# The first third of a modulation matrix walked by column halves, with a query projection cut in two around it

## The reference, cut to what matters

```
mod = silu(cond) @ w_ada + b_ada              # cond: 2 rows (prompt, sample); w_ada: 2048 x 12288
sh1, sc1, gt1, sh2, sc2, gt2 = split(mod, 6)  # 2048 columns each
h = rmsnorm(x, g_pre_mix) * (1.0 + sc1) + sh1
proj = h @ w_in                               # q, k, v, g, decay ranks, hyena inputs
q = proj[:, 0:512]
```

## Time and profile before

| | us |
|---|---|
| three runs | 1532.54, 1532.09, 1527.59 |
| median | 1532.09 |
| profiled execution, its own time | 1530.56 |
| its span | 1528.7 |
| PE busy in the span | 1379.7 (90%) |
| DVE busy | 748.8 (49%) |
| ACT busy | 241.7 (16%) |
| DMA moved | 422.19 MB |
| mean granted TensorE clock | 0.965 of full speed |

### The profile page before, as it was taken

How to read it: one execution, slowest core, us unless ns; L and a number is a source line. 1 busy time by engine, 2 the same in 40 slices (tenths; PEclk the granted TensorE clock), 3 DMA queues, 4 the chain that set the end, 5 groups by cost and what they waited for, 6 DMA issues and landing times.

```text
span 1528.7 us, 14045 instructions
## 1 busy us (share of the span) xinstructions
PE 1379.7 (90%) x5198; PEld 630.9 (41%) x5198; DVE 748.8 (49%) x1269; ACT 241.7 (16%) x401; POOL 75.1 (5%) x126
## 2 busy tenths in 40 slices
PE   2679999999999989999999999889989888798977
PEld 0135544444555545555544444543333333333322
DVE  0139889998677687978693752530000000000006
ACT  2110320100011111211121101521111101111104
POOL 3010000000001000000000001000000000000001
PEclk9689999999999999999999999989999999999999
DMA  9998458777549643322215844589999999999996
GB/s 345 424 359 254 170 173 276 249 259 254 165 144 339 222 146 109 117 69 90 83 55 213 289 157 170 235 351 427 427 426 394 430 427 428 426 386 427 427 424 279
DMA packets 134032, 422.19 MB, mean 276 GB/s; under 512 B 10253, under 2 KB 76024, under 8 KB 116852
## 3 DMA queue, kind: packets, MB, share of 16 engines
q1 hardware_dynamic: 120292, 375.79, 64.3%
q0 software_dynamic: 7584, 33.38, 6.0%
q10 hardware_dynamic: 6096, 12.20, 2.2%
HBM read 407.96 MB, written 22.58 MB: 282 GB/s over the span
## 4 chain that ended last, share of the span: by engine, by line
PE 74%; DMA 11%; DVE 8%; issue 3%; ACT 2%; ACTq 0%; POOL 0%; DVEq 0%; SPq 0%; POOLq 0%
PE ps L503 19%; PE ps L506 19%; PE ps L892 13%; PE ps L912 7%; DMA s_mem<-in_w_exp_gate 4%; PE ps L777 3%; DMA s_mem<-in_w_ada 3%; DMA s_mem<-in_w_exp_down 2%; DVE s_mem L1766 2%; PE ps L450 2%; PE ps L674 1%; DMA s_mem<-in_hy_freq 1%; PE ps L625 1%; PE ps L432 1%; DVE s_mem L1738 1%
## 5 line engine op out<-in xcount | busy, mean ns | idle before, releaser
L1592 DVE SCALAR_TENSOR_TENSOR s_mem<-s_mem,s_sT 128x512 f32<-128x512 f32 x480 | 339.4, 748 | 32.6 <-DMA s_mem<-in_w_ada 16.2
L503 PE MATMUL ps<-s_mem 128*128 128x384 f32 x1024 | 342.5, 492 | 1.1 <-DVE s_mem L1623 1.1
L506 PE MATMUL ps<-s_mem 128*128 128x512 f32 x672 | 292.8, 594 | 0.7 <-ACT s_mem L1366 0.7
L892 PE MATMUL ps<-s_mem 128*64 128x512 f32 x1152 | 256.4, 602 | 19.9 <-DMA s_mem<-in_w_exp_gate 18.7
L503 PEld LDWEIGHTS ps<-s_mem 128*128 128x128 f32 x1024 | 193.3, 191 | 142.5 <-issue 18.0
L506 PEld LDWEIGHTS ps<-s_mem 128*128 128x128 f32 x672 | 126.3, 190 | 158.5 <-issue 157.6
L892 PEld LDWEIGHTS ps<-s_mem 128*64 128x64 f32 x1152 | 87.4, 139 | 185.9 <-issue 185.9
L2059 DVE TENSOR_TENSOR s_mem<-s_mem,ps 64x512 f32<-64x512 f32 x18 | 12.2, 679 | 296.3 <-ACT s_mem L1461 296.3
L912 PE MATMUL ps<-s_mem 128*64 128x512 f32 x576 | 144.2, 659 | 9.3 <-DVE s_mem L2061 9.3
L1262 ACT ACTIVATE s_mem<-ps 128x512 f32<-128x512 f32 (+1 forms) x61 | 34.4, 581 | 316.3 <-PE ps L506 154.0
L912 PEld LDWEIGHTS ps<-s_mem 128*64 128x64 f32 x576 | 43.7, 150 | 96.4 <-issue 84.6
(11 more groups left out here) (287 smaller groups left out, 1025.0 us busy)
## 6 DMA issues: line engine op xcount, KB each, us to landing
s_mem<-in_w_ada SPq DMA_DIRECT2D x256, 256.0 KB, 3.2
s_mem<-in_w_exp_gate SPq DMA_DIRECT2D x32, 2048.0 KB, 21.1
s_mem<-in_w_exp_up SPq DMA_DIRECT2D x32, 2048.0 KB, 25.4
s_mem<-in_w_exp_down SPq DMA_DIRECT2D x32, 2048.0 KB, 24.4
s_mem<-in_w_in SPq DMA_DIRECT2D x24, 2048.0 KB, 8.8
s_mem<-in_w_ada SPq DMA_DIRECT2D x16, 2048.0 KB, 12.5
s_mem<-in_w_out SPq DMA_DIRECT2D x8, 2048.0 KB, 8.2
y_slots<-s_mem ACTq DMA_DIRECT2D x34, 256.0 KB, 11.1
```

Source lines behind the costliest of these rows:

```text
L503: m = mm(ps[:, banks[m_], 0:TOK], v[:, k, m_ * P:(m_ + 1) * P], hT[:, kk, :], start=(kk == 0), stop=(kk == KT - 1))
L506: m = mm(ps[:, banks[m_], :], hT[:, kk, m_ * P:(m_ + 1) * P], v[:, k, :], start=(kk == 0), stop=(kk == KT - 1))
L892: m = mm(ps[half, 0, :], hgT[:, kh * 8 + k, :], weights(e, 2 * kh + which)[:, k, :], start=(kh + k == 0), stop=(kh * 8 + k == KT - 1), ski ...
L1592: v.op(ve.scalar_tensor_tensor(out=o, in0=w, scalar=scale, in1=o, op0=ALU.mult, op1=ALU.add), S("piece_used") if last else None)
```

## The change

The first third of `w_ada` is loaded as 16 blocks of 512 rows by 1024 columns, so 4 KB in a piece per row instead of 16. The first eight (`ada_step(0, i)`) hold columns 0 to 1023 of scale and of shift, alternating, and complete the modulation of channel tiles 0 to 7; the second eight (`ada_step(1, i)`) do tiles 8 to 15. A step still has 8 matmuls of 32 columns.

The row work on DVE is replaced: ACT copies the sums out of PSUM (`ada_copy`), PE brings them into columns with 16 matmuls of 128x32 against a constant (`ada_columns`), and DVE adds bias and gain there in three small instructions and modulates 8 tiles (`modulate`).

The first half of the query projection (8 of 16 channel tiles, 32 matmuls) is spread among the second eight steps, from buffers of its own (`wq`); the second half (32 matmuls) follows `ada_columns(1)`. SP issues the two query blocks after ring loads 7 and 12. Eight pieces of the later thirds are issued after ring loads 9 to 15, and 12 steps of `ada_steps` run before `modulate(1)`. Before the decay ranks there are now 12 + 4 + 2 steps on DVE instead of 26; six of the steps taken away return inside GLA heads 0, 1 and 3 (two each) and two before the heads. ACT's queue now issues the condition rows and x first and the filter MLP's small inputs after them.

The core of the diff:

```diff
-            slot = i % RING if i < KT else (i - KT + 1) % 2
+            slot = i % RING if i < 8 else i % 2
...
+        Q_LOAD_AFTER = {7: 0, 12: 1}
...
+            def ada_step(g, i):
+                r, q = i // 2, (SCALE, SHIFT)[i % 2]
+                cols = q * D + g * 2 * NCOL
+                w = next_slot(pe, w_ada[4 * r * P:4 * (r + 1) * P, cols:cols + 2 * NCOL].rearrange("(k p) n -> p k n", p=P))
...
+            for i in range(4, 8):
+                for kt in range(4 * (i - 4), 4 * (i - 3)):
+                    x_turn(kt)
+                ada_step(0, i)
...
+            ada_columns(0)
+            pe.wait_ge(S("in_q0"), 16)
+            for m_ in range(4):
+                take(pe, m_, f"q_{m_}", ("act",))
+                if m_ < 3:
+                    q_products(m_, range(8))
+                    ada_step(1, 2 * m_)
+                    ada_step(1, 2 * m_ + 1)
+            q_products(3, range(2))
+            ada_step(1, 6)
+            q_products(3, range(2, 4))
+            ada_step(1, 7)
+            q_products(3, range(4, 6))
+            ada_columns(1)
+            q_products(3, range(6, 8))
+            pe.wait_ge(S("in_q1"), 16)
+            for m_ in range(4):
+                q_products(m_, range(8, KT)).then_inc(filled(f"q_{m_}"), 1)
...
-            run(26)
...
+            modulate(0)
+            sine_argument("hid2", 1, P)
+            run(12)
+            modulate(1)
+            run(4)
+            run(2)
...
-            run(4)
+            run(6)
...
-                    run((2, 1, 2, 1, 1, 1, 2, 2)[event])
+                    run((2, 2, 2, 2, 1, 1, 2, 2)[event])
```

More of the change, by code:

```diff
@@ L77, in shape_constants @@
     lower = (np.arange(P) >= BLK)[:, None]
-    base = np.concatenate([ident, tri, sel.reshape(P, 2 * P), total, np.tile(rows, (P, 1)), tokens, lower], 1).astype(np.float32)
+    conds = np.zeros((P, 2, 32), np.float32)
+    for j in range(4):
+        for c in range(2):
+            conds[32 * j + c, j // 2, c] = 1
+    base = np.concatenate([ident, tri, sel.reshape(P, 2 * P), total, np.tile(rows, (P, 1)), tokens, lower, conds.reshape(P, 64)], 1).astype(np.float32)
     masks = np.zeros((P, 2, P), np.int32)
@@ L435, in ada_sum, with ada_columns @@
                 mi.then_inc(filled(key), 1)
[L437 to L454, removed]
+            def ada_step(g, i):
+                r, q = i // 2, (SCALE, SHIFT)[i % 2]
+                cols = q * D + g * 2 * NCOL
+                w = next_slot(pe, w_ada[4 * r * P:4 * (r + 1) * P, cols:cols + 2 * NCOL].rearrange("(k p) n -> p k n", p=P))
+                bank, key = (6 if g == 0 else 4) + q, f"ada{g}{q}"
+                if r == 0:
+                    take(pe, bank, key, ("act",))
+                for kk in range(4):
+                    k = 4 * r + kk
+                    for h in range(2):
+                        j = 2 * h + k % 2
+                        m = mm(ps[32 * j:32 * j + 32, bank, :], sT[:, k, :], w[:, 2 * kk + h, :], start=(k < 2),
+                               stop=(k >= KT - 2), skip_group_check=True)
+                slot_done(m, key if r == 3 else None)
+            def ada_columns(g):
+                bank, key = 6 if g == 0 else 4, f"cols{g}"
+                for q in range(2):
+                    wait_read(pe, "act", f"ada{g}{q}")
+                take(pe, bank, key)
+                for q in range(2):
+                    for i in range(8):
+                        at_ = 32 * (8 * q + i)
+                        m = mm(ps[:, bank, at_:at_ + 32], ada_rows[:, q, i % 4 * P:(i % 4 + 1) * P], conds[:, i // 4, :],
+                               start=True, stop=True, skip_group_check=True)
+                m.then_inc(filled(key), 1)
             def x_turn(kt):
@@ L999, in _ @@
                 if i == 0:
-                    small_loads()
-                for _ in range(PIECES_AFTER.get(i - KT, 0)):
+                    sp.dma_start(base[:, :], T["k_base"]).then_inc(S("in_base"), 16)
+                if i in Q_LOAD_AFTER:
+                    load_q(Q_LOAD_AFTER[i])
+                for _ in range(PIECES_AFTER.get(i, 0)):
                     load_piece()
@@ L1222, in _ @@
                 load(dst, src, "in_mlp")
-            for t in range(NT):
-                load(x_sb[:, t, :], x_rows[t], "in_x")
             wait_read(act, "dve", "colA")
```

187 lines of the change are left out of this document (100 added, 87 removed).

## The result

| | runs | median, us | ratio to before | 95% interval |
|---|---|---|---|---|
| changed kernel, first comparison | 4 | 1543.49 | 1.0090 | 1.0073 to 1.0106 |
| changed kernel, on another occasion (`e0_after_again`) | 5 | 1543.81 | 1.0079 | 1.0066 to 1.0092 |

The changed kernel is slower by 0.8 to 0.9%, 12 to 14 us; 1541 us was forecast. The profiled execution took 1542.97 us, its span is 1541.1 us, 12.4 us more than the span of before. The mean granted clock is 0.966 (before 0.965).

A forecast was written before the change was run, and what follows sets the result against it. The prediction took DMA bytes to bound the early stage, then PE's chain. Later projection end 7.9 us, chunk 7 wait 1.8 and heads 1.0 sum to 10.7 on 1530.56, giving 1541.3 us; range 1530 to 1548.

The forecast's parts named there:

- What bounds the stage: Early stage bound by DMA bytes: share near 1.00 to about 125 us, 360 to 380 GB/s from 60 to 120 us.
- (a): Landing of the first eight blocks: eighth block at 57.8 us, with 0.6 us taken for rows of 4 KB.
- (b): Second eight blocks ahead of the last landing, 16.78 MB: 41.1 us.
- (c): Two query blocks and seven pieces ahead of the last block, 7.86 MB at 345 GB/s: 22.8 us, lower bound 19.6.
- (d): POOL's small transfers, 0.92 MB, falling ahead of the last block: 3.6 us of all DMA engines.
- second rival: Whole kernel: short rows go at nearly full rate and nothing waits on DVE; 1532 us, no measurable change; chance 0.23.
- From the landing to the end of the projection: Last block's step, columns, DVE work and remaining query products: 31.6 us; projection ends at 156.9, 7.9 us later.
- The moved steps: DVE, eight steps behind, is 11.8 us late against a slack of 10.0; PE waits about 1.8 us at chunk 7.
- The heads: DVE's extra steps inside the GLA heads: 0.3 us a head, 1.0 us in all (0 to 3).
- the faster rival: Pieces and POOL's transfers don't delay the blocks; last block lands at 108.3, kernel takes 1521 to 1524 us; chance 0.10.

The follow-up runs named there:

- e0_after_again: Changed kernel measured once more with no edit, on another occasion: 1543.81 us, ratio 1.0079 to before.
- e4_q1_behind: Changed kernel with the load of the query weights' second half behind the last column block instead of three blocks earlier: 1536.14 us, ratio 1.0044 to before.
- e2_pool_late: Changed kernel with POOL's first 0.92 MB of transfers behind the last modulation block: 1542.02 us, ratio 1.0082 to before.
- e3_steps_back: Changed kernel with DVE's eight steps back ahead of the decay ranks and the head loop's steps as before: 1539.01 us, ratio 1.0067 to before.
- e5_before_18_steps: Kernel before with only the order of DVE's steps, the pieces and chunk 8's sum as in the changed kernel: 1533.57 us, ratio 1.0019.
- e1: Changed kernel with the loads of the seven early pieces left out, so its output is not the reference's: 1549.28 us, ratio 1.0126 to before.
- e8: Changed kernel with the edits of e2_pool_late, e3_steps_back and e4_q1_behind together: 1530.08 us, ratio 0.9995 to before.
- e6: Changed kernel with all first-half query products behind the second half's column matmuls, not between the blocks: 1561.09 us, ratio 1.0212 to before.
- e7: Changed kernel with the edits of e2_pool_late and e4_q1_behind, four early pieces, six late DVE steps: 1528.92 us, ratio 0.9992; again (e7_again) 1529.28 us, 0.9993.
- e9: Against e7: all 26 DVE steps ahead of the input projection, none late, head steps as before the change: 1531.49 us, ratio 1.0009 to before.
- e10: Against e7: two more DVE steps ahead of the input projection, so four are late instead of six: 1530.01 us, ratio 1.0002 to before.

## Why the prediction held, and where it did not

1. **What bounds the stage.** Right. DMA is full to 123 us, at 377 GB/s from 60 us on, as forecast, and each thing moved behind the last block brings the landing forward (5.2 us for the query block, 3.2 for three pieces, 2.0 for POOL).
2. **(a) the eighth block.** 57.8 forecast, 55.95 measured. Rows of 4 KB go at 407 GB/s, within the bounds. More than in the gap of 24 to 30 us (382 GB/s for 367, 0.2 us) was gained from 12 to 24 us, where x and the small rows come in another order (376 for 339 GB/s, 1.1 us); the forecast had left that stretch as it was.
3. **(b), (c), (d).** 67.5 us forecast, 67.45 measured, from 55.95 to 123.40, by two errors that cancel. (b) at 407 GB/s is 41.2. (c) was mis-sized: a query block went at 403 GB/s (`e4_q1_behind`), two are 10.4 us, and the pieces' 3.67 MB take 9.3 us at the 393 of the mixture, 19.7 us and not 22.8 (an estimate; the rate of pieces alone no window shows). Taking the seven pieces away brought 8.1 us. So (d) and what came with it took 6.5 us, not 3.6: around POOL's packets the rate is 305 and 307 GB/s, and `e2_pool_late` shows that part of that time would be a gap anyway. The Trainium skill, DMA: Bandwidth & Descriptors, section Specifications, with full rate from 512 B on, came nearer to (c) (19.0) than my two windows of 341 and 350 GB/s. These I had misread: they were not full. Where DMA is full with such short rows its share reads 1.05, so a mean of 1.00 hides a gap. Parts of the same two windows of the kernel before:

```profile
129.20:130.60 1.40, 1.40 (x6) 0.87 (x5) 1.30 (x3) 0.00 (x0) 0.00 (x0) 1.00 0.72 148
131.00:136.00 5.00, 5.00 (x17) 2.94 (x16) 4.76 (x7) 0.49 (x1) 0.00 (x0) 1.00 1.05 395
152.20:153.40 1.20, 0.48 (x5) 0.17 (x2) 0.95 (x2) 0.49 (x1) 0.00 (x0) 1.00 0.65 149
156.00:160.00 4.00, 2.69 (x8) 0.90 (x6) 1.75 (x4) 2.17 (x4) 0.00 (x0) 1.00 1.06 389
```

Without the gaps the mixture goes at 389 to 395 GB/s in the kernel before as in the changed one (393), and (c) would have been 7.86 MB at 390, 20.2 us. What spoke against the second rival was this gap.

4. **From the landing to the end of the projection.** 31.6 us forecast, 29.1 measured. The last step ran at the full clock (1.92 us; I had taken 3.6), and DVE's part was hidden (1.2). `ada_columns` took 3.65 for 3.8. The projection ends 3.5 us late, not 7.9: this is the first term that was mis-sized.
5. **The moved steps.** The mechanism was right, the size was the second mis-sized term. 1.8 us forecast at chunk 7; 3.4 measured at chunks 6 and 7, and 1.65 for the granted clock behind the wait, which I had not priced at all. `e3_steps_back` takes all of it back, `e5_before_18_steps` makes 1.93 and 1.70 of it alone. Most of the excess in the wait is 1.35 us in which DVE itself idled ahead of chunk 7; its timeline in the changed kernel:

```profile
342.58 0.89 DVE L1626 TENSOR_SCALAR s_mem<-s_mem,s_sT 128x512 f32<-128x512 f32 x2 [1.35 <-PE ps L432]
```

The profile names PE's sum of chunk 6, which had just ended. But in the code this step waits for the sum of chunk 3, long done, and for its piece of `w_ada`, and at the same place `e2_pool_late` and `e4_q1_behind` show 1.17 and 0.83 us for DMA. So DVE waited for a piece here, too, by this reading; no run takes this wait away alone.

6. **The heads.** 1.0 forecast, 0.5 measured.
7. **The second low clock, near 797 us, 2.5 us.** Not forecast. It stands in seven of the fourteen traces (changed, `e0`, `e1`, `e2`, `e3`, `e5`, `e8`) and not in the other seven (before, `e4`, `e6`, both of `e7`, `e9`, `e10`). The waits around it, 1.71 us, 0.20 and 0.67, are the same in either group. It does not go with the late steps (`e3` and `e8` have none). What decides it stays open, and with it whether these 2.5 us belong to the change.

The sum came out (1541 for 1543.5) because 4.4 us too much before 153 us met 3.3 us too little at chunk 7 and 2.5 at 797; the rest (0.4 at the k projection, 0.7 in the experts, 0.9 less in and behind the heads) is small. The rival of short rows had the rows right and "nothing waits on DVE" wrong, and so its time; the faster rival needed a landing before 113 us, and `e7_all` at 112.6 shows that even this gives level and not faster: of 7.0 us at the end of the projection 2.8 are left at 790 us.

## What to carry to other kernels

When products are spread among loads that set the time, count everything that gets in front of the last load, and move behind it what is not needed with it: here the second weight half (5.2 us) was the cheapest to move. An engine from which work is taken early, because "there is time later", should be followed to the next place where another engine needs its result; here that was 210 us further on and cost 5.1 us at the first state update, where all that stood ahead of the query projection's end had cost 3.5 net. A mean DMA share over ten microseconds can hide a gap: look at the slices before taking its rate as a price. And a wait of 2 to 3 us on TensorE should be priced with the low clock behind it, here another 1.6 to 1.7 us.

## What I had not expected of the hardware

The granted clock after short waits near chunk 7, from the profiles (the same work: the six instructions behind the chunk's sum):

| wait ahead, us | kernel | same work behind it, us (2.84 at full clock) |
|---|---|---|
| 1.31 (DMA) | `e7_again` | 2.84 |
| 1.72 | `e6_products_behind` | 2.84 |
| 1.93 | `e5_before_18_steps` | 4.54 |
| 1.97 | `e1_no_early_pieces` | 4.02, and the chunk sum 1.53 instead of 1.06 |
| 2.35 (DMA) | `e10_four_late` | 4.54 |
| 2.53 | `e4_q1_behind` | 3.54, and the chunk sum 1.92 instead of 1.06 |
| 2.82 | `e2_pool_late` | 4.54 |
| 3.03 | `e0_after_again` | 4.35, and the chunk sum 1.19 instead of 1.06 |
| 3.04 | changed | 4.36, and the chunk sum 1.19 instead of 1.06 |

Each fall costs 1.56 to 1.70 us, whatever the length of the wait before it. The wait of 1.80 us ahead of chunk 6 in `e4_q1_behind` was followed by none (chunk sum 1.06, the 48 instructions behind 20.87). Near 797 us the same short waits stand in the traces with a fall and in those without. In the early stage the wait alone does not tell either: the last step of `e1_no_early_pieces` ran at a low clock behind a wait of 1.98 us (2.79 us), that of the changed kernel at full clock behind 3.21 (1.92 us).
